# mLSTM head of a two-block kernel: a fourth block in the joint product, packed gates, splits in another order

## What is computed

```python
def mlstm_mixer(u, w_in, conv_w, conv_b, gate_b, w_out):
    z = u @ w_in
    qk = silu(causal_conv(z[..., :2 * A_QK], conv_w, conv_b))
    v = z[..., 2 * A_QK:2 * A_QK + A_V]
    og = z[..., 2 * A_QK + A_V:2 * A_QK + 2 * A_V]
    gates = z[..., 2 * A_QK + 2 * A_V:] + gate_b
    ...
    ig = gates[..., :A_HEADS]
    lf = log_sigmoid(gates[..., A_HEADS:])
    hs = mlstm_scan(q, k, v, ig, lf)
    y = from_blocks(hs) * sigmoid(og)
    return y @ w_out
```

## Time and profile before

| | us |
|---|---|
| median of 3 runs | 800.76 |
| lowest and highest | 799.43, 803.1 |
| the profiled execution's own time | 797.87 |
| its span, first to last instruction | 796.1 |

### The profile page before, as it was taken

The page is one execution under the profiler, slowest core; times in us unless marked ns, Lnnn a source line. Parts: engine busy times, 40 slices in busy tenths (PEclk is TensorE's granted clock), DMA queues, the critical chain, the costliest instruction groups (busy, mean ns, idle before and its releaser), DMA issues.

```text
span 796.1 us, 14522 instructions
## 1 busy us (share of the span) xinstructions
PE 782.0 (98%) x5744; PEld 735.3 (92%) x5744; DVE 572.2 (72%) x907; ACT 415.0 (52%) x729; POOL 116.3 (15%) x136
## 2 busy tenths in 40 slices
PE   9999999999989999899999999999999999999997
PEld 9999999999989999689999998879999988999985
DVE  6777676699676976487877777986577667467763
ACT  7544444454247566385444443455655557456541
POOL 3700000032220000000000000010054411035510
PEclk9999999999999999999999999999999999999999
DMA  9876666695478653368777678664865571754531
GB/s 345 293 266 235 218 246 244 217 326 179 15 164 287 193 168 104 105 217 290 286 255 249 214 262 309 206 225 61 258 217 154 145 259 44 245 182 126 162 111 53
DMA packets 52290, 161.94 MB, mean 203 GB/s; under 512 B 11376, under 2 KB 12912, under 8 KB 52224
## 3 DMA queue, kind: packets, MB, share of 16 engines
q1 hardware_dynamic: 52224, 161.02, 62.2%
HBM read 159.91 MB, written 1.09 MB: 202 GB/s over the span
## 4 chain that ended last, share of the span: by engine, by line
PE 85%; DMA 5%; DVE 5%; issue 2%; ACT 1%; SPq 0%; POOL 0%; DVEq 0%; POOLq 0%; ACTq 0%
PE ps L351 22%; PE ps L353 22%; PE ps L352 21%; DMA raw<-wst 3%; PE ps L715 3%; PE ps L771 3%; PE ps L772 3%; PE ps L773 3%; DMA adr<-wada 2%; DVE w L1157 2%; PE ps L577 1%; PE ps L686 1%; DVE acc L1175 1%; PE ps L705 1%; ACT w L820 1%
## 5 line engine op out<-in xcount | busy, mean ns | idle before, releaser
L1157 DVE TENSOR_TENSOR w<-raw,w 128x1024 fp32r<-128x1024 f32 x237 | 287.7, 1224 | 143.8 <-ACT w L820 143.3
L351 PE MATMUL ps<-u,w 128*128 128x256 f32 (+1 forms) x1283 | 367.7, 287 | 1.5 <-DVE g L1404 1.0
L353 PE MATMUL ps<-u,w 128*128 128x256 f32 (+1 forms) x1283 | 364.4, 284 | 0.0
L352 PE MATMUL ps<-u,w 128*128 128x256 f32 (+1 forms) x1283 | 363.8, 284 | 0.0
L820 ACT CAST w<-raw 128x1024 fp32r<-128x1024 f32 x237 | 245.9, 1050 | 129.0 <-PE ps L353 84.0
L351 PEld LDWEIGHTS ps<-u,w 128*128 128x128 f32 x1283 | 242.0, 189 | 8.2 <-issue 4.3
L353 PEld LDWEIGHTS ps<-u,w 128*128 128x128 f32 x1283 | 242.2, 189 | 0.0
L352 PEld LDWEIGHTS ps<-u,w 128*128 128x128 f32 x1283 | 241.4, 188 | 0.1
L1175 DVE SCALAR_TENSOR_TENSOR acc<-adr,cact,acc 128x1024 f32<-128x1024 f32 x42 | 55.6, 1340 | 5.6 <-DMA adr<-wada 5.6
L1843 POOL TENSOR_SCALAR Sb<-Sb,st 128x256 f32<-128x256 f32 x32 | 44.8, 1413 | 96.5 <-DVE st L1612 96.5
L1829 POOL TENSOR_TENSOR rst<-sst,eps 128x1 f32<-128x1 f32 x8 | 4.4, 555 | 326.0 <-DVE sst L1671 326.0
(11 more groups left out here) (254 smaller groups left out, 965.5 us busy)
## 6 DMA issues: line engine op xcount, KB each, us to landing
raw<-wst SPq DMA_DIRECT2D x245, 512.0 KB, 4.8
adr<-wada SPq DMA_DIRECT2D x48, 512.0 KB, 4.2
sq<-weight_rows SPq DMA_DIRECT2D x4, 512.0 KB, 6.6
Bt<-bias_rows SPq DMA_DIRECT2D x8, 192.0 KB, 4.8
hT<-xT SPq DMA_DIRECT2D x4, 272.0 KB, 4.6
g2row<-weight_rows SPq DMA_DIRECT2D x2, 512.0 KB, 7.1
outT<-hT SPq DMA_DIRECT2D x4, 256.0 KB, 2.0
cs<-cst SPq DMA_DIRECT2D x1, 140.0 KB, 5.9
```

What stands on the lines that cost most here:

```text
L351: e.matmul(out, a, x1, start=first, stop=False)
L352: e.matmul(out, a, x2, start=False, stop=False)
L353: return e.matmul(out, b, x1, start=False, stop=last)
L1157: e.tensor_tensor(b, raw[:, k % NRAW, :], a.bitcast(F32), ALU.subtract).then_inc(*tick(s_split, k))
```

## The change

1. **Packed gates.** Of chunk 66 only the first 64 columns of each 128 hold anything. The upper part of these now goes into columns 0 to 63 and the lower part into columns 64 to 127 of one `w1` (`packed`), so that one matmul with `u1` and one with `u2` make both products; VectorE adds the two halves of the result (`t1`, `t2`).
2. **A fourth block in the head.** v 1 joins the gates, qk 0 and v 0; its chunk is now number 69 and qk 1's number 70. The head takes all four banks, and qk 1 takes bank 7 (`spare`).
3. **Splits behind the head in another order.** ScalarE's split of chunk 70 (`C_A + NW - 1`) moves from behind all eight casts of `u1` to behind the second. Chunk 71 and the following are split at other places of both engines' programs.
4. **Sums of 64 columns.** `column_sums` multiplies by 64 equal columns where it had one.
5. **Output chunks.** The splits of chunks 95, 96 and 97 stand ahead of the outputs of heads 5, 6 and 7, no longer behind all three.
6. **Row operations.** In VectorE's `weighed`, `rows(1, 1)` comes ahead of four `lower(0, k)`.

```diff
+        def packed(x):
+
+            y = x.rearrange("p (k h c) -> p k h c", h=2, c=64)
+            return y[:, :, 0, :], y[:, :, 1, :]
...
-            rot, uses = [0], [0] * 8
+            rot, spare, uses = [0], [], [0] * 8
...
             def place(key, b=None):
 
                 if b is None:
-                    b = rot[0] % 4
-                    rot[0] += 1
+                    b = spare.pop() if spare else rot[0] % 4
+                    rot[0] += b < 4
...
-                            m = products(ps[:, b, 0:n], c + j, kt, x1[:, kt, :], x2[:, kt, :], False, True)
+                            if c + j == C_A:
+                                w = PLACE[c][0][:, o:o + P]
+                                e.matmul(ps[:, b, 0:n], w, x1[:, kt, :], start=False, stop=False)
+                                m = e.matmul(ps[:, b, 0:n], w, x2[:, kt, :], start=False, stop=True)
+                            else:
+                                m = products(ps[:, b, 0:n], c + j, kt, x1[:, kt, :], x2[:, kt, :], False, True)
...
                     for j, b in enumerate(b_):
                         e.matmul(ps[:, b, 0:n], PLACE[c + j][0][:, o:o + P], x1[:, kt, :], start=i == 0, stop=False)
-                        e.matmul(ps[:, b, 0:n], PLACE[c + j][1][:, o:o + P], x1[:, kt, :], start=False, stop=False)
+                        if c + j != C_A:
+                            e.matmul(ps[:, b, 0:n], PLACE[c + j][1][:, o:o + P], x1[:, kt, :], start=False, stop=False)
...
+                spare.append(7)
+
+            def column_sums(b, src, n, w, col, first, last):
...
+                    many = wts[:, w[0]:w[1]].unsqueeze(2).broadcast_to([P, w[1] - w[0], 64])
+                    o = 128 * j + col
+                    m = e.matmul(ps[0:z - a, b, o:o + 64 * (w[1] - w[0])], src[:, a:z], many, start=first and j == 0,
+                                 stop=last, skip_group_check=True)
...
-                keys = [("gates",)] + [(x, j) for j in range(8) for x in ("qk", "v")]
-                head(keys[:3], c, x1, x2, T, *u_of("a"))
+                head([("gates",), ("qk", 0), ("v", 0), ("v", 1)], c, x1, x2, T, *u_of("a"))
                 for j in range(8):
                     if j:
-                        block(("qk", j), c + 1 + 2 * j, x1, x2, T)
-                        block(("v", j), c + 2 + 2 * j, x1, x2, T)
+                        block(("qk", j), c + 1 + 2 * j + (j == 1), x1, x2, T)
+                        if j > 1:
+                            block(("v", j), c + 2 + 2 * j, x1, x2, T)
                         v_transpose(j - 1)
...
+                    a, r = PLACE[k][0], raw[:, k % NRAW, :]
+                    if k == C_A:
+
+                        a, r = packed(a)[0], packed(r)[0]
+                    e.copy(a, r).then_inc(*tick(s_upper, k))
...
                 for k in range(KT):
                     e.wait_ge(*(read(("r2", s)) if k == KT - 1 else (s_tmp.handle, at(s_tmp, (s, k)))))
                     e.copy(u1[:, k, 0:n], tmp[:, k % 4, 0:n]).then_inc(*tick(s_u1, ("a", k)))
+                    if k == 1:
+                        split_to(C_A + NW - 1)
...
             def mlstm():
                 c = C_A
+
+                split_to(c + NW)
                 e.wait_ge(s_zero.handle, 1)
-                split_to(c + NW - 1)
...
+                    split_to(c + 2 + 2 * j + NW - 1)
+                    for h in ((0, 1), (), *((h,) for h in range(2, 8)))[j]:
+                        proj(("v", h))
+                        if h > 1:
+                            e.wait_ge(s_vtr.handle, at(s_vtr, h - 2))
+                        e.copy(vT[:, h % 2, :], out_of(("v", h), T)).then_inc(*reading(("v", h)))
...
                 for h in (5, 6, 7):
+
+                    split_to(c + 24 + h)
                     output(h)
                 split_to(c + 32)
...
+                    (a, b), r = PLACE[k], raw[:, k % NRAW, :]
+                    if k == C_A:
+                        (a, b), r = packed(a), packed(r)[0]
+                    e.tensor_tensor(b, r, a.bitcast(F32), ALU.subtract).then_inc(*tick(s_split, k))
...
+                split_to(c + NW - 1)
                 e.wait_ge(s_spread.handle, at(s_spread, ("r2", "f0")))
                 e.memset(zp[:, :, 0:3], 0.0).then_inc(*tick(s_zero, 0))
-                split_to(c + NW - 1)
...
-                e.tensor_copy(fx_, ps[32:40, b, 0:T]).then_inc(*reading(("gates",)))
+                e.tensor_copy(fx_, ps[32:40, b, 0:T])
+                split_to(c + NW)
+                e.tensor_copy(t1, ps[64:72, b, 0:T])
+                e.tensor_copy(t2, ps[96:104, b, 0:T]).then_inc(*reading(("gates",)))
...
-                        e.tensor_scalar(fx_, fx_, vc[0:8, V_GB + 1:V_GB + 2], None, ALU.add).then_inc(*tick(s_gate, "f"))
+                        e.tensor_tensor(gi, gi, t1, ALU.add).then_inc(*tick(s_gate, "i+"))
+                        e.scalar_tensor_tensor(fx_, fx_, vc[0:8, V_GB + 1:V_GB + 2], t2, ALU.add, ALU.add).then_inc(
+                            *tick(s_gate, "f"))
...
+                    split_to(c + 2 + 2 * j + NW - 1)
                     if j:
-                        split_to(c + 2 + 2 * j + NW - 1)
                         v_copied(j - 1)
...
                 for h in (5, 6, 7):
+                    split_to(c + 24 + h)
                     output(h)
                 lower(7)
                 split_to(c + 32)
...
                 rows(1, 0)
+                rows(1, 1)
                 for k in range(4, KT):
                     lower(0, k)
-                rows(1, 1)
...
     qkv = np.stack([cols(aw[:, 0:1024]), cols(aw[:, 1024:2048])], 1).reshape(16, P, CH)
+    qkv = qkv[[0, 1, 3, 2, *range(4, 16)]]
```

More of the change, by code:

```diff
@@ L249, in build @@
         W_ONE, W_TWO, W_FFN = (0, 1), (1, 2), (2, 4)
-        SUM_Y, SUM_G, SUM_C = (0, 2, 4), (1, 3, 5), (0, 1, 2)
+        SUM_Y, SUM_G = 0, 64
         COL = [(0, 0, 0, 256, 128), (368, 368, 112, 256, 128), (256, 624, 240, 256, 16)]
@@ L394, in head @@
                         e.matmul(ps[:, b, 0:n], PLACE[c + j][0][:, o:o + P], x2[:, kt, :], start=False, stop=False)
-            def column_sums(b, src, n, w, cols, first, last):
-                tt = sum_tiles(n)
-                for j, (a, z) in enumerate(tt):
-                    m = e.matmul(ps[0:z - a, b, cols[j]:cols[j] + w[1] - w[0]], src[:, a:z], wts[:, w[0]:w[1]],
-                                 start=first and j == 0, stop=last, skip_group_check=True)
+                spare.append(7)
+            def column_sums(b, src, n, w, col, first, last):
+                for j, (a, z) in enumerate(sum_tiles(n)):
+                    many = wts[:, w[0]:w[1]].unsqueeze(2).broadcast_to([P, w[1] - w[0], 64])
+                    o = 128 * j + col
+                    m = e.matmul(ps[0:z - a, b, o:o + 64 * (w[1] - w[0])], src[:, a:z], many, start=first and j == 0,
+                                 stop=last, skip_group_check=True)
                 return m
@@ L498, in ffn_out @@
                 place(("sumc", s), 5)
-                column_sums(5, hyg[:, 1, :], n, W_TWO, SUM_C, True, False)
-                column_sums(5, sqa[:, 2, :], n, W_TWO, SUM_C, False, True).then_inc(*tick(s_colsum, ("sumc", s)))
+                column_sums(5, hyg[:, 1, :], n, W_TWO, SUM_Y, True, False)
+                column_sums(5, sqa[:, 2, :], n, W_TWO, SUM_Y, False, True).then_inc(*tick(s_colsum, ("sumc", s)))
             def both_scales(s, n):
@@ L819, in split_to @@
                         e.wait_ge(s_proj.handle, at(s_proj, last_of[BEFORE[k]]))
-                    e.copy(PLACE[k][0], raw[:, k % NRAW, :]).then_inc(*tick(s_upper, k))
+                    a, r = PLACE[k][0], raw[:, k % NRAW, :]
+                    if k == C_A:
+                        a, r = packed(a)[0], packed(r)[0]
+                    e.copy(a, r).then_inc(*tick(s_upper, k))
             def proj(key):
@@ L1155, in split_to @@
                     e.wait_ge(s_upper.handle, k + 1)
-                    a, b = PLACE[k]
-                    e.tensor_tensor(b, raw[:, k % NRAW, :], a.bitcast(F32), ALU.subtract).then_inc(*tick(s_split, k))
+                    (a, b), r = PLACE[k], raw[:, k % NRAW, :]
+                    if k == C_A:
+                        (a, b), r = packed(a), packed(r)[0]
+                    e.tensor_tensor(b, r, a.bitcast(F32), ALU.subtract).then_inc(*tick(s_split, k))
             def proj(key):
@@ L1233, in first_input @@
                 e.wait_ge(s_colsum.handle, at(s_colsum, ("sum", "x")))
-                e.tensor_scalar(sst[:, 0:2], ps[:, 7, 0:4:2], EPS, None, ALU.add)
-                e.tensor_scalar(sst[0:16, 2:3], ps[0:16, 7, 4:5], EPS, None, ALU.add).then_inc(*reading(("sum", "x")))
+                e.tensor_scalar(sst[:, 0:2], ps[:, 7, 0:256:128], EPS, None, ALU.add)
+                e.tensor_scalar(sst[0:16, 2:3], ps[0:16, 7, 256:257], EPS, None, ALU.add).then_inc(*reading(("sum", "x")))
                 e.wait_ge(*read(("sum", "x")))
@@ L1323, in first_scale @@
```

(4 more changed lines are left out.)

10 lines of the change are left out of this document (2 added, 8 removed).

## The result

| | before | after |
|---|---|---|
| median of 12 runs, us | 800.38 | 803.37 |
| lowest to highest, us | 796.14 to 803.1 | 800.8 to 805.66 |
| the profiled execution's own time, us | 797.87 | 802.59 |
| its span, us | 796.1 | 800.8 |

The account below looks back on a forecast made before the run. TensorE, busy 98% of the span, was taken as the bound. Terms 7.3 - 3.3 - 0.5 + 0.1 = +3.6 us gave 801.5 us on the profiled execution, 804.4 us as median; range 792 to 808 us.

Parts of the forecast that it names:

- The head, +7.3: mLSTM head: six u1 casts queue behind chunk 70's late landing, so qk 2 starts at 244.0 instead of 236.75 us.
- The half clock: In the head: after over 10 us idle, TensorE comes back at half the clock for 3.4 us.
- the bound of 5.5 without a fall: Lower bound for the head: if the clock does not fall, qk 2 starts at 242.3 us, +5.5 us.
- The output chunks, -3.3: Output products: chunk 95 split earlier, so TensorE no longer stands 3.16 us before the matmul at 328.24 us; -3.3 us.
- rows(1, 1), -0.5: Transposes at 349.16 us: their 0.40 us wait goes, as the row operation precedes four subtractions; -0.5 us.
- The sums, +0.1: Boundary before the head: 64-column sums cost at most 0.012 us more per record, 18 ahead of the stores; +0.1 us.
- The gates' copies at nothing: Behind the head: VectorE's packed split, two copies and one addition lie under TensorE's qk 1 and cost nothing.
- the early case: Chunk 70 lands early in the head, making the kernel faster: 792.4 or 794 us; chance 0.17.
- The early rival: Chunk 70 in by 217.8 us: qk 2 starts at 232.0 us, -8.4 us in all, 792.4 or 794 us; chance 0.17.
- The rival that chunk 95's split would be late: Output products: no gain there, so +6.9 us, 807.7 us; chance 0.03.

Follow-up runs that it names:

- e6_tail_undone: Changed kernel with the splits of chunks 95 to 97 back behind the last heads' outputs and rows(1, 1) back behind the four subtractions: 806.84 us, ratio 1.0107.
- the filler run: Changed kernel plus 84 dense matmuls nothing reads, on TensorE behind the head's second step, where it waits for chunk 70's cast: 800.20 us, ratio 1.0029.
- e2_stores_75: Changed kernel with the four element-wise stores behind the load of chunk 74 instead of chunk 69: 791.95 us, ratio 0.9921.
- e4_both: Changed kernel with the stores behind chunk 74's load and chunk 70's cast behind all eight casts of u1: 791.76 us, ratio 0.9923.
- e8_sums_1col: Changed kernel with stores behind chunk 74's load, chunk 70's cast behind all u1 casts, and sums of one column: 790.90 us, ratio 0.9911.
- e11_three_blocks: Kernel before with stores behind chunk 74's load, chunks 95 to 97 split between outputs, rows(1, 1) ahead, and 64-column sums: 792.77 us, ratio 0.9932.
- e10_before_tail_stores: Kernel before with stores behind chunk 74's load, chunks 95 to 97 split between outputs, rows(1, 1) ahead; one-column sums kept: 791.99 us, ratio 0.9930.
- e3_before_stores_75: Kernel before with only the four stores moved behind the load of chunk 74: 797.46 us, ratio 0.9993.

## Why the prediction was right, and where it was off

**The head, +7.3.** Right by its steps. The cast of chunk 70 stood between two casts of `u`, released by `raw`; TensorE was empty from 221 to 231 us; the clock was at half when it came back; SP's next load went out at 238.96 us. From the wait's end to qk 2 were forecast 230.66 to 244.0, 13.34 us, and measured 13.42. The term came out as +8.24: 0.9 us from a wait that ended later (the landing at 230.13 us, for the load went out 1.04 us later, behind sums and a store's issue that took longer). The landing is the uncertain part: 226.8 to 230.1 us in the executions with the stores ahead of it. Where it came 2 us earlier (e6_tail_undone, 228.0 us) the head was 2.2 us shorter.

**The half clock.** 3.4 us at half was assumed, 3.9 us measured; the filler run puts its price at 1.9 us, where the prediction had 1.8 (7.3 less the bound of 5.5 without a fall).

**A wrong name.** The prediction has v 0 wait for chunk 70 before the change. The chunk is v 1's there (66 the gates, then qk and v by turns); the sums speak of v 1 and qk 2, so no number hangs on it.

**The output chunks, -3.3.** Right: -3.44, and undoing them brought the wait back. What the prediction did not see is that such a wait can be followed by half the clock, and then costs 5 us.

**rows(1, 1), -0.5.** Right: -0.62, and the undone kernel has the 0.40 us wait again.

**The sums, +0.1.** Mis-sized. The 18 records ahead of the stores take 2.20 us for 1.79, +0.41: 0.023 us each, about twice the bound that was taken from records of 129 columns. The 24 in the boundary take 3.28 us for 2.66, another +0.62, which was not in the sum; that came back, since the clock no longer fell: from the first of these sums to the head it is 6.89 us after and 6.91 before.

**The gates' copies at nothing.** Wrong, and the one step whose mechanism failed. "The packed split, the two copies and one addition for the gates lie on VectorE while TensorE works on qk 1" named TensorE as the cover. But with the copies VectorE and ScalarE become the chain that ends last behind the head, up to the heads' outputs 50 to 60 us later: +1.4 us. The unpacked kernel shows it gone, and all fourteen traces agree: from qk 2 to the first output product the seven with packed gates take 79.04 to 79.28 us, the seven without 77.58 to 77.71.

So the terms sum to +8.2 - 3.4 - 0.6 + 1.4 = 5.6 us, and the trace has 4.7. Of the missing 0.9 us, 0.7 is the wait at 524.94 us that before had and after did not. The medians differ by 3.0 us. That the forecast came within 1 us of the time is therefore in part luck: the head and the copies cost 2.4 us more than the sum had, 0.9 us came back where no term stood, and the medians differ by 1.7 us less than the two profiled executions. The range of 792 to 808 us took in the early case as well, so that the time fell into it says little; the steps seen in the traces say more.

**The early rival.** It was the right mechanism under the wrong condition: move the stores and it comes true, 791.95 us. By its own sum it would have been 8.4 us under before; measured against before beside it 6.3 us (0.9921 of 797.9), in part because it left out the gates' copies too; and it had qk 2 at 232.0 us, where that trace has it at 234.14. The rival that chunk 95's split would be late is out.

## What to carry to other kernels

Before a wait is moved forward in an engine's program, look at what it waits for and at everything that stands behind it in that program: a late DMA that only its reader felt becomes a stop for all. Two small edits cured it about equally well here (792.52 and 791.95 us): the wait put back behind the other work, and one number on another queue, in SP's program, which put four small stores behind five loads. And "hidden behind TensorE" is only free if the engine that does the work is not itself the next chain: follow it to where TensorE next waits for it, even 50 us on.

## What the runs showed of the hardware

- **Stores by single elements.** Four stores of 1024 numbers, 4 KB each, three of them issued directly ahead of it, held a 512 KB load on the same queue for 19 to 21 us; without them ahead it landed in 4.0 us. In the changed kernel's trace the stretch of 205 to 232 us holds 3595 packets, 3167 of them under 512 bytes, and moves 66 GB/s. The Trainium skill ("DMA: Bandwidth & Descriptors", Why small descriptors are slow) names fixed costs per packet and per descriptor as the reason that small ones are slow; the traces agree in direction (in e2_stores_75 a store of 4 KB took 12.8 to 18.8 us to land). No run here separates that cost from others: from 216 to 226 us no packet under 512 bytes starts any more in the changed kernel's trace, and it still moves only 30 GB/s. What holds the loads in that time is open.
- **The clock can fall while TensorE is busy.** In all five profiled executions with sums of one column it fell to half (1.2 GHz) around the end of the 24 in the boundary, at 213.2 to 214.7 us (for 3.41 us in three, 6.83 us in two), though TensorE had been busy 9.08 of the 9.1 us from 204.0 to 213.1. In the nine with 64 columns, busy 9.10 of 9.1 us, it did not fall at that place. Two pairs differ in the sums alone: e4_both and e8_sums_1col, e11_three_blocks and e10_before_tail_stores.
- **One wait, two prices.** The 3.43 us from start to start at the output products were followed by the full clock in one trace (before) and by 3.41 us at half in two (e3_before_stores_75, e6_tail_undone), the same instructions around them. In both the clock was still full in the wait and fell behind it, 0.2 to 0.4 us into the work.
